# Query norms of a hybrid attention layer: squares of six query tiles of a half folded to 32 channels a head, high and low part summed by one product instead of two

## The chip, the cores and the metric

The kernel runs on one core of a Trainium2 chip. The metric is the device time of one execution in microseconds. TensorE is called PE, VectorE DVE, ScalarE ACT, GpSimd POOL and SyncE SP below; a core has one of each, and each works through its own instructions in order, waiting on semaphores where it needs another.

## The reference, cut to what matters

One layer: 16 meta tokens are put in front of 1024 frames of width 2048, normalised, and multiplied by one input projection of 5376 columns. The queries (16 heads of 64 channels) and keys (2 heads) get an RMSNorm per head, then go into chunked windowed attention; beside it runs a pooling mixer; both are gated and multiplied by an output projection.

```
def _rmsnorm(x, g):
    xf = x.astype(jnp.float32)
    y = xf * lax.rsqrt(jnp.mean(xf * xf, axis=-1, keepdims=True) + EPS)
    return (y * g.astype(jnp.float32)).astype(x.dtype)
...
    q = _rmsnorm(q.reshape(b, l, N_KV_HEADS, GQA_GROUP, HEAD_DIM), q_norm_g)
```

The change touches only the mean over the 64 channels of each query head inside this norm.

## The kernel before, in words

Channels lie on the partitions and frames along the free axis. The frames are worked in two halves of 512 (`h` = 0, 1). In a half, PE computes the projection in tiles of 128 output channels by 512 frames: first keys and values, then the eight query tiles (`PAIRS`, two heads each, called t = 0 to 7 here), then four groups in which attention and the pooling mixer run between further projection tiles. After both halves comes the output projection, which is the second large stage of PE's work.

Every fp32 operand of a product is split into a high part that the fp32r format holds and a low part that is the rest, and a product is the sum of three: high by high, high by low, low by high. The weights arrive in blocks of 128 x 512; a query tile takes four blocks (`TILE_BLKS`), and a block is 12 matmuls (`tile`, lines 1470, 1471, 1477). ACT makes a block's high part (`split_high`, line 630, into `wh`), DVE the low part (`split_low`, line 979, into `wl`), three blocks ahead (`LEAD`), in four buffers, so that the split of block s+3 waits until PE has finished block s-1.

The order of everything in the query stage is written out by hand, on each engine by a loop over s = 0 to 32. Turn s is the turn of block s; the query tile t ends with block 4t+3. What belongs to the norm of tile t hangs on these turns:

- ACT, turn 4t+4: `q_square` reads the finished tile from its PSUM bank twice and writes the squares in fp32 (`q_sq`) and rounded to fp32r (`q_sqh`, in the buffer `d_h`).
- DVE, turn 4t+4, ahead of its `split_low`: `square_low` writes the low part, `q_sq` less `q_sqh`, to `q_sql` (in `d_l`).
- PE, behind block 4t+4: `sum_squares` (lines 1610 and 1611) multiplies both parts by the matrix of ones `ones_r` (it lies in `pw_h`), into the bank `PT` or, for odd t, `PM` (a half of `OP`). A matrix of two 64 x 64 squares of ones gives each channel the sum over its head.
- DVE, turn 4t+5: `q_mean`. ACT, the same turn: `q_sqrt`. DVE, turn 4t+6: `q_norm`, a reciprocal and a product.

PE waits for the low part in front of its sum, and everything behind that wait on PE waits too:

```
                    pe.wait_ge(s_qsl, h * PAIRS + t + 1)
```

Other steps share these turns: on DVE `k_norm` in turn 4 (a reciprocal and one or two products for the keys) and `k_band` in turns 11, 15, 19 and 23 (low parts of the keys); on ACT `k_band` in turns 7 and 14, `v_all_out` in turn 10; on PE the transposes `v_windows` behind block 8, which need `q_norm` of tile 0. Tile 7 is finished in the first turns of the first group.

Of the kernel before, what the change touches and what calls it, by code (L numbers as in the profile page):

```python
# [15 lines left out]
P = 128  # L16
# [15 lines left out]
HD = 64  # L32
PAIRS = 8
# [17 lines left out]
IN_BLKS = KV_BLKS + Q_BLKS + GROUPS * G_BLKS  # L51
ROWT = HALF // P
UNITS = 4

FIRST_SPLITS = ({3: (1, 2), 7: (3, 4), 11: (5, 6), 15: (7,)},
                {3: (3,), 7: (4,), 11: (5, 6), 15: (7,)})
# [27 lines left out]
C_ID, C_BLK, C_MASK = 0, 128, 256  # L84
# [9 lines left out]
def hymba_layer(nc, xcat, norm_g, w_in, w_out, pool_w, vecs, consts, out):  # L94
    f32, f32r, bf16 = mybir.dt.float32, mybir.dt.float32r, mybir.dt.bfloat16
    ACT = mybir.ActivationFunctionType
    ALU = mybir.AluOpType
# [3 lines left out]
    with ctx:  # L101
# [3 lines left out]
        def sem(name):  # L105
            return ctx.enter_context(nc.semaphore(name))
# [8 lines left out]
        cst = sb("cst", [P, C_N])  # L115
# [30 lines left out]
        pw_h = sbi("pw_h", [P, BLK], f32r)  # L146
# [10 lines left out]
        scr = sbi("scr", [P, 7168])  # L157
# [52 lines left out]
        q_sq = [scr[:, 1056:1568], scr[:, 1568:2080]]  # L210
# [3 lines left out]
        q_sqh = [d_h[:, 0, :], d_h[:, 1, :]]  # L214
        q_sql = [d_l[:, 0, :], d_l[:, 1, :]]
        ones_r = pw_h[:, 0:P]
        q_rs = [scr[:, 2080:2592], scr[:, 2592:3104]]

        prob = scr[:, 0:QUAD * KEYS].rearrange("p (c k) -> p c k", c=QUAD)
# [18 lines left out]
        QB = [S[:, 0, :]] + [(R[1][:, :], R[0][:, :], O)[t % 3] for t in range(PAIRS - 1)]  # L238
# [58 lines left out]
        s_pvl = sem("s_pvl")  # L297
        s_qsq = sem("s_qsq")
        s_qsl = sem("s_qsl")
        s_qss = sem("s_qss")  # L300
        s_qsd = sem("s_qsd")
        s_qrs = sem("s_qrs")
# [69 lines left out]
        ME = [ONE + 2 * GROUPS * (h + 1) for h in range(HALVES)]  # L372
        OE = [ONE + GROUPS * UNITS * (h + 1) for h in range(HALVES)]

        OUT_UNITS = HALVES * GROUPS * UNITS

# [29 lines left out]
        def _(sp):  # L406
# [15 lines left out]
            def spill(q):  # L422

                sp.wait_ge(s_me, ONE + 2 * (q + 1))
                sp.wait_ge(s_oe, ONE + UNITS * (q + 1))
                for t in (2 * q, HK + 2 * q):
# [201 lines left out]
        def _(act):  # L628
# [49 lines left out]
            for h in range(HALVES):  # L678
# [104 lines left out]
                def q_square(t):  # L783
                    product_done(act, h, KV_BLKS + t * TILE_BLKS)
                    if t >= 2:
                        act.wait_ge(s_qss, h * PAIRS + t - 1)
                    for dst in (q_sq[t % 2], q_sqh[t % 2]):
                        nc.scalar.activation(dst, QB[t], ACT.Square).then_inc(s_qsq, 1)

                def q_sqrt(t):  # L790
                    if t >= 2:
# [4 lines left out]
                def qdiag(u, g):  # L796

                    act.wait_ge(s_s, ONE + 2 * ((h * GROUPS + g) * UNITS + u))
                    q = mixed[:, bass.ds(PAIRS + g * 2 + u // 2, 1),
# [7 lines left out]
                for s in range(Q_BLKS + 1):  # L807
                    if s and s % 4 == 0:
                        q_square(s // 4 - 1)
                    if s < Q_BLKS:  # L810
                        split_high(h4 + KV_BLKS // RAW, s + LEAD)
                    if s == 0:
                        k_square()
                    if s == 2:
                        r_rows()
                    if s == 3:
                        k_sqrt()
                    if s > 4 and s % 4 == 1:
                        q_sqrt(s // 4 - 1)
                    if s == 10:  # L820
                        v_all_out()
                    if s in (7, 14):
                        k_band((s - 7) // 7)
                    if s == 23:
                        v_operand(0)
                    if s == 30:
                        qdiag(0, 0)
# [139 lines left out]
            for n in range(OUT_BLKS):  # L967
                p, s = divmod(n, PASS)
# [8 lines left out]
        def _(dve):  # L977
# [30 lines left out]
            for h in range(HALVES):  # L1008
# [72 lines left out]
                def k_band(e, i):  # L1081
                    src = slice(e * HD, (e + 1) * HD)

                    high = band_h[src, e, :].rearrange("p (c n) -> p c n", n=BAND)
                    dve.wait_ge(s_kbh, 8 * h + (2, 8)[e])
                    for dst in (slice(i * HD, (i + 1) * HD),):
                        low = band_x[dst, e, :].rearrange("p (c n) -> p c n", n=BAND)
                        sub(low[:, :, 0:CHUNK], kT[src, :].rearrange("p (c n) -> p c n", n=CHUNK),
                            high[:, :, 0:CHUNK])
                        ins = sub(low[:, :, CHUNK:BAND],  # L1090
                                  k_meta[src, :].unsqueeze(1).to_broadcast([HD, NCH + 1, META]),
                                  high[:, :, CHUNK:BAND])
                    if e == 1 and i == 1:
                        ins.then_inc(s_kbl, 1)

                def v_operand(e):
                    dve.wait_ge(s_vh, 3 * (h * KVH + e + 1))
                    sub(v_s[:, :, 1, :], v_all[:, :, e * HD:(e + 1) * HD], v_s[:, :, 0, :])
                    sub(vm[64:64 + META, 0, :], vm_all[:, e * HD:(e + 1) * HD], vm[0:META, 0, :]).then_inc(s_vl, 1)

                def square_low(t):
                    dve.wait_ge(s_qsq, 2 * (h * PAIRS + t + 1))
                    sub(q_sql[t % 2], q_sq[t % 2], q_sqh[t % 2]).then_inc(s_qsl, 1)
# [20 lines left out]
                    sub(qs[HD:P, :, 1, :], q[HD:P], qs[HD:P, :, 1, :]).then_inc(s_qdl, 1)  # L1124

                for s in range(Q_BLKS + 1):
                    if s and s % 4 == 0:
                        square_low(s // 4 - 1)
                    if s < Q_BLKS:
                        split_low(h4 + KV_BLKS // RAW, s + LEAD)  # L1130
                    if s == 1:
                        k_square_low()
                    if s == 3:
                        k_mean()
                        v_out()
                    if s == 4:
                        k_norm()
                    if s > 4 and s % 4 == 1:
                        q_mean(s // 4 - 1)
                    if s > 4 and s % 4 == 2:  # L1140
                        q_norm(s // 4 - 1)
                    if s in (11, 15, 19, 23):
                        k_band((s - 11) // 8, (s - 11) // 4 % 2)
                    if s == 25:
                        v_operand(0)
                    if s == 31:
                        qdiag(0, 0)
# [272 lines left out]
            for i in range(ROWT):  # L1420
                for p in range(PASSES):
                    at = p * PASS + i
# [31 lines left out]
        def _(pe):  # L1454
            mm = nc.tensor.matmul
# [105 lines left out]
            for h in range(HALVES):  # L1561
# [41 lines left out]
                def sum_squares(t):  # L1603
                    pe.wait_ge(s_qsl, h * PAIRS + t + 1)
                    if t == 0:
                        pe.wait_ge(s_ksd, SPANS_BY[h + 1])
                    if t >= 2:
                        pe.wait_ge(s_qsd, h * PAIRS + t - 1)
                    bank = (PT, PM)[t % 2][:, :]
                    mm(bank, ones_r, q_sqh[t % 2], start=True, stop=False)  # L1610
                    mm(bank, ones_r, q_sql[t % 2], start=False, stop=True).then_inc(s_qss, 1)

                def q_events(s):
                    if s == 1:
                        r_transposes()
                    elif s == 2:
                        k_squares()
                    elif s == 8:
                        v_windows()
                    if s and s % 4 == 0:  # L1620
                        sum_squares(s // 4 - 1)

                for t in range(PAIRS):
# [117 lines left out]
            for n in range(OUT_BLKS - LAST):  # L1741
                p, s = divmod(n, PASS)
# [116 lines left out]
```

## Time and profile before

| what | value |
|---|---|
| median of 3 runs | 1175.71 us (1174.88 to 1175.95) |
| the profiled execution's own time | 1175.75 us |
| its span in the trace | 1173.6 us |
| PE busy | 1168.7 us |
| DVE busy | 890.2 us |
| ACT busy | 616.1 us |
| query stage of the first half, by PE's blocks | about 41 to 139 us of the span |

The span is the time from the first to the last instruction in the trace; the execution's own time is 2.1 us more. Busy times are sums over the instructions of an engine. Matmuls overlap: one of 128 x 512 shows 0.39 us, and the next starts about 0.23 us behind it.

### The profile page before, as it was taken

The page shows a single profiled execution, that of the slowest core. Times are in us where ns is not written, and L with a number is a line of the kernel's source. Part 1 is how long each engine was busy: PE and PEld are TensorE (multiplying, and loading weights), DVE is VectorE, ACT ScalarE, POOL GpSimd, SP SyncE. Part 2 cuts the span into 40 slices and gives each one's busy share as a digit, 9 for nine tenths or more (in the row PEclk, how much of TensorE's full clock was granted, in tenths as well). Part 3 has the DMA queues.
Part 4 walks back from the last instruction along what each step waited for, and adds up shares of the span by engine and source line. Part 5 has one row for each costly group of instructions (what it writes and reads, how often), then busy time and mean ns, then how long its engine had stood idle before and what let it go on. Part 6 is the DMA issues. An engine that isn't in the chain of part 4 may idle for free.

```text
span 1173.6 us, 17331 instructions
## 1 busy us (share of the span) xinstructions
PE 1168.7 (100%) x5906; PEld 993.6 (85%) x5906; DVE 890.2 (76%) x1548; ACT 616.1 (53%) x1400; POOL 115.5 (10%) x133
## 2 busy tenths in 40 slices
PE   9999999999999999999999999999999999999999
PEld 8888898898998988888888888888888888888887
DVE  5677878787786885677787787887977977657676
ACT  5654466554665656544564655555654444444442
POOL 0000011030040220000020030220400000200001
PEclk9999999999999999999999999999999999999999
DMA  7255339465385423435268372493246544653443
GB/s 258 82 161 179 90 88 227 121 200 191 120 186 162 126 81 118 156 113 175 88 138 177 90 241 73 102 221 86 85 141 221 167 133 135 187 176 123 142 145 135
DMA packets 85775, 171.41 MB, mean 146 GB/s; under 512 B 8496, under 2 KB 12208, under 8 KB 85552
## 3 DMA queue, kind: packets, MB, share of 16 engines
q1 hardware_dynamic: 72288, 129.21, 35.9%
q0 software_dynamic: 13120, 40.90, 14.2%
q8 instruction: 45, 0.74, 0.3%
q14 instruction: 34, 0.28, 0.1%
q10 hardware_dynamic: 288, 0.28, 0.1%
HBM read 157.77 MB, written 46.14 MB: 174 GB/s over the span
## 4 chain that ended last, share of the span: by engine, by line
PE 99%; DVE 0%; ACT 0%; issue 0%; ACTq 0%; DVEq 0%
PE R L1470 18%; PE R L1471 18%; PE R L1477 18%; PE R L1777 3%; PE R L1778 3%; PE R L1776 3%; PE S L1777 2%; PE S L1778 2%; PE S L1776 2%; PE OP L1777 2%; PE OP L1778 2%; PE OP L1776 2%; PE S L1645 1%; PE OP L1669 1%; PE OP L1477 1%; PE OP L1471 1%
## 5 line engine op out<-in xcount | busy, mean ns | idle before, releaser
L979 DVE TENSOR_TENSOR wl<-raw,wh 128x512 fp32r<-128x512 f32 x384 | 283.4, 739 | 197.8 <-ACT wh L630 196.0
L630 ACT ACTIVATE wh<-raw 128x512 fp32r<-128x512 f32 x384 | 241.0, 629 | 351.5 <-PE R L1477 160.4
L1470 PE MATMUL R<-act_h,wh 128*128 128x512 f32 (+5 forms) x1056 | 380.5, 365 | 0.0
L1471 PE MATMUL R<-act_l,wh 128*128 128x512 f32 (+5 forms) x1056 | 378.5, 364 | 0.0
L1477 PE MATMUL R<-act_h,wl 128*128 128x512 f32 (+5 forms) x1048 | 362.1, 365 | 0.0
L1471 PEld LDWEIGHTS R<-act_l,wh 128*128 128x128 f32 x1056 | 198.5, 188 | 28.6
L1470 PEld LDWEIGHTS R<-act_h,wh 128*128 128x128 f32 x1056 | 198.3, 188 | 28.7
L1477 PEld LDWEIGHTS R<-act_h,wl 128*128 128x128 f32 x1048 | 188.2, 188 | 32.2
L885 ACT ACTIVATE row_buf<-scr 128x512 f32<-128x512 f32 x32 | 20.2, 632 | 79.5 <-DVE scr L1241 79.5
L1183 DVE TENSOR_REDUCE scr<-S 128x288 f32<-128x576 f32 x56 | 42.3, 756 | 25.2 <-PE S L1645 24.3
L1776 PE MATMUL R<-wh,mix_h 128*128 128x512 f32 x152 | 59.1, 389 | 0.0
L1777 PE MATMUL R<-wl,mix_h 128*128 128x512 f32 x152 | 59.1, 389 | 0.0
L1778 PE MATMUL R<-wh,mix_l 128*128 128x512 f32 x152 | 59.1, 389 | 0.0
L1113 DVE RECIPROCAL scr<-scr 128x512 f32<-128x512 f32 x16 | 53.5, 3347 | 0.0
L859 ACT ACTIVATE scr<-scr,nmax 128x144 f32<-128x144 f32 x128 | 51.2, 403 | 3.3 <-DVE nmax L1191 3.3
L600 POOL TENSOR_TENSOR scr<-scr 128x513 f32<-128x513 f32 (+6 forms) x40 | 50.3, 1257 | 3.1
L592 POOL TENSOR_TENSOR scr<-scr,row_buf 128x512 f32<-128x512 f32 (+4 forms) x16 | 20.9, 1304 | 268.3 <-ACT scr L630 258.0
L1776 PE MATMUL S<-wh,mix_h 128*128 128x512 f32 x112 | 43.6, 389 | 0.0
L1777 PE MATMUL S<-wl,mix_h 128*128 128x512 f32 x112 | 43.6, 389 | 0.0
L1778 PE MATMUL S<-wh,mix_l 128*128 128x512 f32 x112 | 43.6, 389 | 0.0
L1776 PE MATMUL OP<-wh,mix_h 128*128 128x512 f32 x104 | 40.5, 389 | 0.0
L1777 PE MATMUL OP<-wl,mix_h 128*128 128x512 f32 x104 | 40.5, 389 | 0.0
(291 smaller groups left out, 1996.2 us busy)
## 6 DMA issues: line engine op xcount, KB each, us to landing
raw<-w_in_blocks SPq DMA_DIRECT2D x271, 256.0 KB, 2.7
wsum<-w_out_in POOLq DMA_DIRECT2D x24, 1024.0 KB, 11.8
raw<-wsum SPq DMA_DIRECT2D x64, 256.0 KB, 2.7
raw<-w_out_in SPq DMA_DIRECT2D x48, 256.0 KB, 3.2
c<-xcat SPq DMA_DIRECT2D x32, 256.0 KB, 3.5
out<-c POOLq DMA_DIRECT2D x28, 256.0 KB, 2.9
mixed<-xcat SPq DMA_DIRECT2D x10, 512.0 KB, 5.5
mx<-mixed SPq DMA_DIRECT2D x8, 512.0 KB, 3.4
```

Of the source, the lines that this page charges most:

```text
L600: ins = pool.tensor_tensor(dst[:, lo:COLS], src[:, lo:COLS], src[:, lo - step:COLS - step], ALU.add)
L630: return nc.scalar.activation(dst, src, ACT.Copy)
L859: nc.scalar.activation(prob[:, c, :], prob[:, c, :], ACT.Exp, bias=nmax[:, c:c + 1], accum_out=den[:, c:c + 1]).then_inc(s_ex, 1)
L979: return nc.vector.tensor_tensor(dst, a, b, ALU.subtract)
L1113: nc.vector.reciprocal(q_rs[t % 2], q_rs[t % 2]).then_inc(s_qrs, 1)
L1183: nc.vector.tensor_reduce(to, both, AX.X, ALU.add).then_inc(s_sm, 1)
L1470: mm(o, wh[:, b, w], xh, start=(k == 0), stop=False)
L1471: mm(o, wh[:, b, w], xl, start=False, stop=False)
L1477: last = mm(o, wl[:, b, w], xh, start=False, stop=(k == KT - 1))
L1776: mm(banks[r], mh, wh[:, slot, :], start=(k == 0), stop=False)
L1777: mm(banks[r], mh, wl[:, slot, :], start=False, stop=False)
L1778: last = mm(banks[r], ml, wh[:, slot, :], start=False, stop=(k == HK - 1))
```

## The change

For the tiles t = 0 to 5 of each half (`FOLDED = 6`) the squares are folded before they are summed. ACT writes the squares of channels 0 to 31 of both heads into a 64-row buffer `q_even`, and those of channels 32 to 63 into another, `q_odd`: four activations of 32 x 512 in place of two of 128 x 512. DVE adds the two (`fold`). ACT copies the 64 x 512 result, rounded to fp32r, into the upper half of `q_sqh` (`fold_high`), and DVE writes the low part into the lower half of the same buffer (`fold_low`). High and low part then lie on the 128 partitions of one operand, and PE takes one product by the matrix `ones_f`, which ACT writes once a half in turn 1 (`ones_folded`). Tiles 6 and 7 stay as they were.

The steps also move: for the folded tiles `fold` and `fold_low` stand in turn 4t+5, PE's sum behind block 4t+5, `q_mean` and `q_sqrt` in turn 4t+6, `q_norm` in turn 4t+7. DVE's `k_band` moves by one turn, to 12, 16, 20 and 24.

```
+FOLDED = 6
...
+        q_even = [q[0:HD] for q in q_sq]
+        q_odd = [scr[0:HD, 5216:5728], scr[0:HD, 5744:6256]]
+        ones_f = pw_h[:, P:2 * P]
...
+                    if t < FOLDED:
+                        for head in range(2):
+                            at = slice(head * 32, (head + 1) * 32)
+                            nc.scalar.activation(q_even[t % 2][at], QB[t][head * HD:head * HD + 32], ACT.Square)
+                            ins = nc.scalar.activation(q_odd[t % 2][at], QB[t][head * HD + 32:(head + 1) * HD], ACT.Square)
+                        ins.then_inc(s_qsq, 2)
+                        return
                     for dst in (q_sq[t % 2], q_sqh[t % 2]):
                         nc.scalar.activation(dst, QB[t], ACT.Square).then_inc(s_qsq, 1)
+
+                def fold_high(t):
+                    act.wait_ge(s_qf, h * FOLDED + t + 1)
+                    copy(q_sqh[t % 2][0:HD], q_even[t % 2]).then_inc(s_qfh, 1)
+
+                def ones_folded():
+                    for to, at in ((0, 0), (32, HD), (HD, 0), (96, HD)):
+                        ins = copy(ones_f[to:to + 32], cst[at:at + 32, C_BLK:C_BLK + P])
+                    ins.then_inc(s_onesf, 1)
...
-                    if s > 4 and s % 4 == 1:
+                    if s == 1:
+                        ones_folded()
+                    if s % 4 == 1 and 0 < s // 4 <= FOLDED:
+                        fold_high(s // 4 - 1)
+                    if s % 4 == 2 and 0 < s // 4 <= FOLDED:
+                        q_sqrt(s // 4 - 1)
+                    elif s % 4 == 1 and s // 4 > FOLDED:
                         q_sqrt(s // 4 - 1)
...
+                def fold(t):
+
+                    dve.wait_ge(s_qsq, 2 * (h * PAIRS + t + 1))
+                    nc.vector.tensor_tensor(q_even[t % 2], q_even[t % 2], q_odd[t % 2], ALU.add).then_inc(s_qf, 1)
+
+                def fold_low(t):
+                    dve.wait_ge(s_qfh, h * FOLDED + t + 1)
+                    sub(q_sqh[t % 2][HD:P], q_even[t % 2], q_sqh[t % 2][0:HD]).then_inc(s_qsl, 1)
...
                 for s in range(Q_BLKS + 1):
-                    if s and s % 4 == 0:
+                    if s % 4 == 0 and s // 4 > FOLDED:
                         square_low(s // 4 - 1)
+                    if s % 4 == 1 and 0 < s // 4 <= FOLDED:
+                        fold(s // 4 - 1)
                     if s < Q_BLKS:
                         split_low(h4 + KV_BLKS // RAW, s + LEAD)
...
-                    if s > 4 and s % 4 == 1:
+                    if s % 4 == 1 and 0 < s // 4 <= FOLDED:
+                        fold_low(s // 4 - 1)
+                    late = s // 4 > FOLDED
+                    if s % 4 == (1 if late else 2) and s > 4:
                         q_mean(s // 4 - 1)
-                    if s > 4 and s % 4 == 2:
+                    if s % 4 == (2 if late else 3) and s > 4:
                         q_norm(s // 4 - 1)
-                    if s in (11, 15, 19, 23):
-                        k_band((s - 11) // 8, (s - 11) // 4 % 2)
+                    if s in (12, 16, 20, 24):
+                        k_band((s - 12) // 8, (s - 12) // 4 % 2)
...
+                    if t < FOLDED:
+                        pe.wait_ge(s_onesf, h + 1)
+                        mm(bank, ones_f, q_sqh[t % 2], start=True, stop=True).then_inc(s_qss, 1)
+                        return
                     mm(bank, ones_r, q_sqh[t % 2], start=True, stop=False)
                     mm(bank, ones_r, q_sql[t % 2], start=False, stop=True).then_inc(s_qss, 1)
...
-                    if s and s % 4 == 0:
+                    if s % 4 == 0 and s // 4 > FOLDED or s % 4 == 1 and 0 < s // 4 <= FOLDED:
                         sum_squares(s // 4 - 1)
```

What this does to the order is best seen in rows. On DVE, in turns 4 and 5 of the first half (tile 0), the kernel before has `square_low` first, then the split of block 7 and the keys' norm (lines 1071 to 1078):

```order
L979 TENSOR_TENSOR d_l<-scr,d_h 128x512 [waits s_qsq]
L979 TENSOR_TENSOR wl<-raw,wh 128x512 [waits s_wh]
L1071 RECIPROCAL scr<-scr 128x528 [waits s_ksd]
L1074 SCALAR_TENSOR_TENSOR k_meta<-scr,vec 128x16 [waits s_krs]
L1078 SCALAR_TENSOR_TENSOR kT<-scr,vec 128x512
L979 TENSOR_TENSOR wl<-raw,wh 128x512 [waits s_wh]
```

The changed kernel has on DVE, in the same two turns, with its own line numbers (1010 is the subtraction, 1135 the fold):

```order
L1010 TENSOR_TENSOR wl<-raw,wh 128x512 [waits s_wh]
L1102 RECIPROCAL scr<-scr 128x528 [waits s_ksd]
L1105 SCALAR_TENSOR_TENSOR k_meta<-scr,vec 128x16 [waits s_krs]
L1109 SCALAR_TENSOR_TENSOR kT<-scr,vec 128x512
L1135 TENSOR_TENSOR scr<-scr 64x512 [waits s_qsq]
L1010 TENSOR_TENSOR wl<-raw,wh 128x512 [waits s_wh]
L1010 TENSOR_TENSOR d_h<-scr,d_h 64x512 [waits s_qfh]
```

What PE's sum waits for stood ahead of the keys' norm and now stands behind it, in two steps with ACT's `fold_high` between them.

On DVE, from turn 11 to 13 of the first half (the norm of tile 1 ends, tile 2's squares begin), the kernel before has:

```order
L979 TENSOR_TENSOR wl<-raw,wh 128x512 [waits s_wh]
L1113 RECIPROCAL scr<-scr 128x512 [waits s_qsd]
L1115 SCALAR_TENSOR_TENSOR mixed<-R,gq,scr 128x512 [waits s_qrs]
L979 TENSOR_TENSOR wl<-raw,wh 128x512 [waits s_wh]
L979 TENSOR_TENSOR band<-kT,band 64x9x64 [waits s_kbh]
L979 TENSOR_TENSOR band<-k_meta,band 64x9x16
L979 TENSOR_TENSOR d_l<-scr,d_h 128x512 [waits s_qsq]
L979 TENSOR_TENSOR wl<-raw,wh 128x512 [waits s_wh] x2
```

The first of these is turn 10's split, and the norm is turn 10's. The changed kernel has on DVE, from turn 11 on:

```order
L1010 TENSOR_TENSOR wl<-raw,wh 128x512 [waits s_wh]
L1153 RECIPROCAL scr<-scr 128x512 [waits s_qsd]
L1155 SCALAR_TENSOR_TENSOR mixed<-R,gq,scr 128x512 [waits s_qrs]
L1010 TENSOR_TENSOR wl<-raw,wh 128x512 [waits s_wh]
L1010 TENSOR_TENSOR band<-kT,band 64x9x64 [waits s_kbh]
L1010 TENSOR_TENSOR band<-k_meta,band 64x9x16
L1135 TENSOR_TENSOR scr<-scr 64x512 [waits s_qsq]
L1010 TENSOR_TENSOR wl<-raw,wh 128x512 [waits s_wh]
L1010 TENSOR_TENSOR d_h<-scr,d_h 64x512 [waits s_qfh]
```

The sequence is the same up to the square's step, but it begins one turn later, with the split of block 14 in place of block 13, and one step of DVE has become two with a wait for ACT between them. Tiles 3, 4 and 5 repeat it.

On ACT, in turns 4 and 5 of the first half (tile 0), the kernel before has:

```order
L788 ACTIVATE scr<-S 128x512 [waits s_blk]
L788 ACTIVATE d_h<-S 128x512
L630 ACTIVATE wh<-raw 128x512 [waits s_blk,s_raw3]
L630 ACTIVATE wh<-raw 128x512 [waits s_blk,s_raw0]
L794 ACTIVATE scr<-scr 128x512 [waits s_qm]
```

The changed kernel has there (799 and 800 are the squares, 639 the copy):

```order
L799 ACTIVATE scr<-S 32x512 [waits s_blk]
L800 ACTIVATE scr<-S 32x512
L799 ACTIVATE scr<-S 32x512
L800 ACTIVATE scr<-S 32x512
L639 ACTIVATE wh<-raw 128x512 [waits s_blk,s_raw3]
L639 ACTIVATE wh<-raw 128x512 [waits s_blk,s_raw0]
L639 ACTIVATE d_h<-scr 64x512 [waits s_qf]
```

Two squares became four, and `fold_high` stands behind both splits, waiting for DVE's fold.

## Rows read from the trace of the kernel before

**Rows 1.** The page: span; busy time, share and count of each engine.

```profile
span 1173.6 us, 17331 instructions
...
PE 1168.7 (100%) x5906; PEld 993.6 (85%) x5906; DVE 890.2 (76%) x1548; ACT 616.1 (53%) x1400; POOL 115.5 (10%) x133
```

**Rows 2.** The waits of PE: line, releaser, us in total, times, longest.

```profile
PE R L1532 <- DVE act_l L991: 0.4, 1, 0.4
```

**Rows 3.** Timeline of PE about block 16 and tile 3's sum: start us, us, instruction.

```profile
86.88 0.39 PE L1470 MATMUL R<-act_h,wh 128*128 128x512 f32 x1
...
89.60 0.39 PE L1610 MATMUL OP<-d_h,pw_h 128*128 128x512 f32 x1
...
90.06 0.39 PE L1470 MATMUL R<-act_h,wh 128*128 128x512 f32 x1
```

**Rows 4.** Timeline of PE behind tile 0, and about `v_windows` behind block 8.

```profile
51.44 0.39 PE L1470 MATMUL R<-act_h,wh 128*128 128x512 f32 x1
...
65.66 0.27 PE L1597 MATMUL R<-cst,v_meta 128*16 128x128 f32 x1
...
66.77 0.50 PE L1610 MATMUL OP<-d_h,pw_h 128*128 128x512 f32 x1
```

**Rows 5.** Timeline of ACT: narrow operations, tile 0's squares, `v_all_out`.

```profile
41.13 0.29 ACT L730 ACTIVATE scr<-xsd 128x128 f32<-128x128 f32 x1
41.33 0.29 ACT L630 ACTIVATE scr<-xrs 16x128 f32<-16x128 f32 x1
...
51.64 0.60 ACT L788 ACTIVATE scr<-S 128x512 f32<-128x512 f32 x1 [0.39 <-PE S L1477]
52.13 0.59 ACT L788 ACTIVATE d_h<-S 128x512 fp32r<-128x512 f32 x1
...
71.04 1.00 ACT L630 ACTIVATE scr<-S 128x1024 f32<-128x1024 f32 x1
```

**Rows 6.** Timeline of DVE in turn 4 of the first half.

```profile
53.36 0.69 DVE L979 TENSOR_TENSOR wl<-raw,wh 128x512 fp32r<-128x512 f32 x1
53.97 3.45 DVE L1071 RECIPROCAL scr<-scr 128x528 f32<-128x528 f32 x1
...
58.26 0.69 DVE L979 TENSOR_TENSOR wl<-raw,wh 128x512 fp32r<-128x512 f32 x1
```

**Rows 7.** Timeline of ACT in turns 14 and 15: splits, and the keys' copies.

```profile
81.70 0.63 ACT L630 ACTIVATE wh<-raw 128x512 fp32r<-128x512 f32 x1 [0.50 <-PE OP L1477]
82.35 0.69 ACT L630 ACTIVATE band<-kT 64x576 fp32r<-64x576 f32 x1
...
84.42 0.63 ACT L630 ACTIVATE wh<-raw 128x512 fp32r<-128x512 f32 x1 [0.25 <-PE OP L1477]
```

**Rows 8.** Timeline of DVE in turns 14 to 16.

```profile
82.97 3.35 DVE L1113 RECIPROCAL scr<-scr 128x512 f32<-128x512 f32 x1
...
87.02 0.68 DVE L979 TENSOR_TENSOR wl<-raw,wh 128x512 fp32r<-128x512 f32 x1
87.73 0.75 DVE L979 TENSOR_TENSOR band<-kT,band 64x576 fp32r<-64x576 f32 x1
...
88.72 0.69 DVE L979 TENSOR_TENSOR d_l<-scr,d_h 128x512 fp32r<-128x512 f32 x1
```

**Rows 9.** The chain between 464 and 467 us: start us, us, what.

```profile
465.39 0.76 DVE act_l L991
```

**Rows 10.** Timeline of PE: its first matmuls, and those behind the wait at 466 us.

```profile
1.47 5.06 PE L1488 MATMUL PT<-pw_l 128*128 128x512 f32 x11 [1.47 <-DVE pw_l L994]
6.33 1.16 PE L1510 MATMUL S<-cst,mixed 128*128 128x128 f32 x8
...
466.19 0.50 PE L1532 MATMUL OP<-act_h,wh 128*128 128x512 f32 x1 [0.17 <-DVE act_l L991]
466.53 0.40 PE L1533 MATMUL OP<-act_l,wh 128*128 128x512 f32 x1
```

**Rows 11.** A stretch: PE, PEld, DVE, ACT, POOL busy; PEclk, DMA share, GB/s.

```profile
0.00:4.00 4.00, 2.53 (x6) 2.05 (x7) 0.48 (x1) 1.51 (x3) 1.50 (x8) 1.00 0.52 148
```

More of the change, by code:

```diff
@@ L299, in hymba_layer @@
         s_qsl = sem("s_qsl")
+        s_qf = sem("s_qf")
+        s_qfh = sem("s_qfh")
+        s_onesf = sem("s_onesf")
         s_qss = sem("s_qss")
```

## The prediction

> **What bounds the kernel now.** The page comes first: PE is busy for 1168.7 of the span's 1173.6 us, DVE for 890.2, ACT for 616.1 [rows 1]. PE's own waits come second: behind its first microseconds the longest is 0.4 us, and the other one there is shorter [rows 2]. So time is won only by taking work from PE, and lost one for one wherever PE must wait, since nothing later on PE has slack that could give a wait back. Third come the timelines of PE, DVE and ACT over the query stage: they show what a product costs, and how late DVE and ACT are when PE asks for the low part of the squares. The profiled execution took 1175.75 us, 0.04 us above the median of the three runs, so the sum below can be set against either.
>
> **What is removed.** Twelve matmuls (tiles 0 to 5 of two halves). The sum of tile 3 begins at 89.60, and the next block at 90.06: two products, 0.23 us each [rows 3]. That it shows 0.39 us is overlap; what counts is from start to start. 12 x 0.227 = 2.7 us, all of it on PE's path. This is the whole possible gain.
>
> **What is added off PE.** For each folded tile ACT has two squares and one 64 x 512 copy more, DVE one subtraction more. None of these lies on PE in itself, but PE's sum waits for the last of them. Their prices: the trace has no 32 x 512 activation. The nearest rows say that time goes by columns and not by partitions: on ACT 16 x 128 and 128 x 128 both take 0.29 us [rows 5], and on DVE 64 x 576 takes 0.75 where 128 x 512 takes 0.69 [rows 6, 8]. So I take full prices: a square 0.49 us from start to start, [rows 5], `fold` and `fold_low` 0.69 us, `fold_high` 0.63 as a 128 x 512 copy (a 64 x 576 one shows 0.69) [rows 7]. The lower bound is that narrow operations cost half: kept for the range. From one engine's end to the next one's start goes 0.03 to 0.04 us: DVE's operation at 465.39 ends at 466.15, and PE starts at 466.19 [rows 9, 10]. Behind such a wait PE's first matmul takes 0.34 us to the next, not 0.23 [rows 10]: 0.11 us more for each wait. The four copies of `ones_folded` (0.2 us each by [rows 5]) fall in front of the split of block 5, three blocks ahead of its use: nothing. The queues of SP and POOL get no new work.
>
> A block is 2.72 us (86.88 to 89.60) [rows 3]. In what follows E is the moment at which PE starts the block behind a tile. PE used to ask for the low part at E + 2.72, and now asks at E + 5.44.
>
> **Tile 0, first half.** E = 51.44 [rows 4], so PE asks at 56.88. ACT starts the squares at 51.64 and has four: 51.64 + 4 x 0.49 = 53.60 [rows 5]. Its split of block 7 ends at 54.23, and DVE's split starts at 54.26. DVE then has the keys' norm, at 54.26 + 0.61 = 54.87; it lasts 4.29 us (53.97 to 58.26) [rows 6], to 59.16. The square's step stood ahead of it; now `fold` stands behind it: 59.16 to 59.85. `fold_high` 59.88 to 60.51, `fold_low` 60.54 to 61.23, PE at 61.27. PE waits 4.39 us. In the second half the keys' norm has no meta columns and is a reciprocal and a product of 512 columns, which elsewhere take 4.05 us (82.97 to 87.02) [rows 8]: 4.15 us.
>
> **Tiles 4 and 5, the plain pattern**, on tile 3's times, E = 86.88, PE asks at 92.32. The norm of the tile before now hangs on turn 4t+3: ACT's split there runs from 84.42 to 85.05 [rows 7], DVE's starts 0.03 later, at 85.08; 0.61 for the split, 4.05 for the norm: 89.74. The split and the keys' band from 87.02 to 88.72 take 1.70 [rows 8]: 91.44. `fold` ends at 92.13, `fold_high` at 92.79, `fold_low` at 93.51, PE at 93.55: a wait of 1.23 us. Before, the norm started one turn earlier, and the low part ran from 88.72 to 89.41 [rows 8], 0.2 us ahead of PE's question at 89.60: the margin was thin already.
>
> **Tiles 2 and 3** add a delay on ACT. A late sum delays `q_mean`, it delays `q_sqrt`, and ACT's turn-10 copies (0.16 + 1.0 us [rows 5]) or turn-14 copies (82.35 to 84.17, 1.8 us [rows 7]) stand behind `q_sqrt` and ahead of the next split, on which DVE's norm hangs. Followed through with the same prices, the split is 0.7 us late for tile 2 and 0.4 us for tile 3: waits of 1.95 and 1.66 us.
>
> **Tile 1** is covered: PE has `v_windows` ahead of its sum, 1.1 us (65.66 to 66.77) [rows 4], and no band work is due; the low part is ready 1.3 us early. But `v_windows` itself needs the norm of tile 0, now in turn 7: PE starts block 7 at 61.27 + 0.34 + 2.72 = 64.33; split on ACT, split on DVE and norm end 5.64 us later at 69.97; PE comes at 69.77 and waits 0.24 us.
>
> **Tile 6** has the old steps, but the norm of tile 5 still ends at E + 2.86 (89.74 less 86.88); `square_low` ends at E + 3.55, PE wanted it at E + 2.72: 0.87 us. Tile 7 is as before.
>
> **The sum.** First half 4.39 + 0.24 + 1.95 + 1.66 + 1.23 + 1.23 + 0.87 = 11.57 us of waiting, and seven restarts at 0.11 = 0.77: 12.3 us. Second half 12.1 us. What the kernel before has of the same kind goes off, about 0.2 us a half (its sum of tile 1 takes 0.33 us to the next matmul). 24.0 - 2.7 = 21.3 us more: 1175.7 + 21.3 = 1197.0 us.
>
> **The clock.** The eleven first matmuls, behind 1.47 us of idleness at the program's start, go from 1.47 to 6.33 us: 0.44 us each, against 0.23 later [rows 3, 10]. These are the durations that the two levels of 1.2 and 2.4 GHz would give, though the granted clock stands at 1.00 there [rows 11]. If PE fell back to that pace behind the two waits of over 4 us, for as many matmuls as at the start, each would cost 11 x (0.44 - 0.23) = 2.4 us. No wait of that length occurs in this trace behind the start, so it can't say. The Trainium skill (TensorE: Matmul & The Clock Gate, "Why this matters for your kernels") tells kernels to leave no long gaps between bursts of matmuls, because the clock then drops to its lower level. By that rule the waits of tile 0, the only long ones, would each be followed by a slow stretch, and the sum would be that of the first rival below; no run here shows it yet.
>
> **The rivals.**
> - *The clock falls too* (0.20). For it speaks the slow start in rows 10; against it that PE is fully busy on both sides of a wait. All of the above plus 2.4 or 4.7 us: 1199.4 to 1201.7.
> - *Narrow operations are cheap* (0.09). If 64 x 512 costs half, `fold`, `fold_high` and `fold_low` save together 1.0 us in each of tiles 0, 2, 3, 4 and 5, in both halves: 10 us less, about 1187. Rows 5 and 8 speak against it.
> - *Not slower* (0.03): PE's wait is not felt, because the low part is there in time after all. That needs `fold` to run ahead of the long DVE operations; then only the removed products count, 1175.7 - 2.7 = 1173.0. It decides where the waits of both halves together stay under 2.7 us, a ninth of what I get; tile 0 alone gives 8.5, and its `fold` stands behind the keys' norm in the program, so I see no way.
> - The forecast itself has 0.68: 1193 to 1199 by itself.
>
> **How the numbers follow.** 1197.0 is the likeliest. A measurement of this kernel tells a change of about 0.2% (2.4 us) from none. Slower by more than that are the forecast, the clock and the cheap case: 0.97. Within: 0.01, faster: 0.02, both out of the third rival. The range, 1191 to 1202, holds the forecast and the clock (0.88) and leaves out the cheap case's centre and the third rival; its lower end allows half of the cheap case's saving (5 us) and a little more for what starts earlier than I followed it.
>
> **What would show it.** PE's waits should have a row for the single product (line 1657) on DVE's `d_h`, ten times or so, over 20 us in all with a longest of 4.2 to 4.4, and one for line 1659 (tile 6) of about 0.9 each half. The product of tile 0 should start at about 61.3 us in place of 54.16, that of tile 3 about 10.7 us later than in the kernel before (2.7 for the block, less 0.7 for three products saved, 8.7 of waits and restarts); stages behind the query stages should keep their lengths. DVE's `fold` of tile 0 should start straight behind the product into `kT`. Blocks behind a wait should still have 0.23 us to a matmul; 0.44 would be the clock. The forecast would be wrong if 64 x 512 operations last near 0.35 us, or if the waits of tiles 2 to 5 fall under 0.5 us.

## The result, and the profile after

The changed kernel takes 1203.16 us (median of six runs, 1202.74 to 1204.6) against 1175.75 us of the kernel before: the ratio is 1.0236, with a 95% interval of 1.0225 to 1.0247. It is 27.4 us slower. The forecast was 1197.0 with a range of 1191 to 1202, so the direction and the waits came as forecast, and the time came out above the range. The profiled execution took 1204.60 us, 28.85 us over that of before.

The page of the changed kernel, span, busy times and granted clock:

```profile
span 1202.5 us, 17365 instructions
...
PE 1173.4 (98%) x5894; PEld 993.7 (83%) x5894; DVE 899.0 (75%) x1560; ACT 640.3 (53%) x1444; POOL 115.5 (10%) x133
...
PEclk9989999999999999899999999999999999999999
```

Beside [rows 1], PE has twelve matmuls fewer (5894 against 5906) and yet is busy 4.7 us longer, with 24 us of new idleness. The clock has a dip in slice 3 and one in slice 17; the two query stages lie there. The waits of PE in the changed kernel (line, releaser, us in total, times, longest), where [rows 2] had nothing over 0.4 us behind the program's start:

```profile
PE PT L1657 <- DVE d_h L1010: 15.3, 6, 4.7
PE OP L1657 <- DVE d_h L1010: 6.3, 4, 1.6
...
PE PT L1659 <- DVE d_l L1010: 1.4, 2, 0.7
PE OP L1718 <- ACT pm L639: 0.8, 1, 0.8
...
PE R L1642 <- DVE mixed L1155: 0.4, 2, 0.2
```

Line 1657 is the single product of a folded tile (even t into `PT`, odd t into `OP`), 1659 the first product of tile 6, 1642 the first value transpose: the places that the forecast named. Ten of the twelve folded tiles make PE wait, tile 1 of each half does not.

Tile 0 of the first half, timeline of DVE:

```profile
54.07 0.69 DVE L1010 TENSOR_TENSOR wl<-raw,wh 128x512 fp32r<-128x512 f32 x1 [3.47 <-ACT wh L639]
...
58.31 0.75 DVE L1109 SCALAR_TENSOR_TENSOR kT<-scr,vec 128x512 f32<-128x512 f32 x1
58.97 0.68 DVE L1135 TENSOR_TENSOR scr<-scr 64x512 f32<-64x512 f32 x1
...
60.34 0.69 DVE L1010 TENSOR_TENSOR d_h<-scr,d_h 64x512 fp32r<-64x512 f32 x1
```

`fold` (line 1135) starts straight behind the product into `kT`, 2.7 us after PE has run out of work. The same place on PE:

```profile
56.00 0.39 PE L1522 MATMUL R<-act_h,wl 128*128 128x512 f32 x1
61.08 0.79 PE L1657 MATMUL PT<-d_h,pw_h 128*128 128x512 f32 x1 [4.70 <-DVE d_h L1010]
61.67 0.63 PE L1515 MATMUL R<-act_h,wh 128*128 128x512 f32 x1
62.10 0.63 PE L1516 MATMUL R<-act_l,wh 128*128 128x512 f32 x1
...
66.37 0.51 PE L1522 MATMUL R<-act_h,wl 128*128 128x512 f32 x1
66.72 0.39 PE L1515 MATMUL R<-act_h,wh 128*128 128x512 f32 x1
```

The next matmul was due at 56.23 and starts at 61.08: 4.85 us lost. (The bracket shows 4.70, because the matmul before it is shown until 56.39; 0.16 us has to be added to every such number.) And then the matmuls stand 0.43 us apart instead of 0.23, for eleven of them. The granted clock in stretches behind it (busy of PE, PEld, DVE, ACT, POOL, then PEclk, DMA share, GB/s):

```profile
51.00:57.00 6.00, 5.39 (x24) 4.13 (x22) 2.93 (x2) 3.50 (x6) 0.00 (x0) 1.00 0.19 61
57.00:61.00 4.00, 0.00 (x0) 0.00 (x0) 3.87 (x6) 1.15 (x2) 0.00 (x0) 0.85 0.00 1
61.00:63.00 2.00, 1.92 (x5) 1.53 (x6) 1.41 (x3) 0.36 (x1) 0.00 (x0) 0.50 0.54 131
...
67.00:70.00 3.00, 3.00 (x15) 2.47 (x14) 2.36 (x2) 2.63 (x6) 0.06 (x1) 1.00 0.17 49
```

1.00 is 2.4 GHz and 0.50 is 1.2 GHz: PE stood still, the clock fell while it did, and came back near 66.4 us. From 61.08 to 66.72 are 5.64 us; at the full clock it would be 0.34 + 12 x 0.227 = 3.06. So 2.6 us are lost to the clock here, and 2.1 us in the same way behind tile 0 of the second half.

Where the 28.85 us lie is seen from equal matmuls. The n-th product of `tile`'s first kind (line 1470 before, 1515 now) is the same work in both kernels; its start in us:

| place | before | changed | later by |
|---|---|---|---|
| start of the first query stage | 38.74 | 38.09 | -0.65 |
| behind it | 141.30 | 155.07 | 13.77 |
| ahead of the second query stage | 481.39 | 495.09 | 13.70 |
| behind it | 586.39 | 614.09 | 27.70 |
| last group, behind the wait on line 1718 | 643.15 | 671.88 | 28.73 |
| near the end of the projections | 853.58 | 882.33 | 28.75 |

The two query stages are 14.42 and 14.00 us longer, and hardly anything (0.07 us) is given back between them.

### The profile page after: what moved, and what is told of

It reads as the page before. It is cut to its first block, busy times and chain, and to the rows that moved or that the text cites. A ratio compares the mean times of both kernels' runs of the same rounds, so it can differ in the third digit from the quotient of the medians.

```text
span 1202.5 us, 17365 instructions
## 1 busy us (share of the span) xinstructions
PE 1173.4 (98%) x5894; PEld 993.7 (83%) x5894; DVE 899.0 (75%) x1560; ACT 640.3 (53%) x1444; POOL 115.5 (10%) x133
## 4 chain that ended last, share of the span: by engine, by line
PE 87%; DVE 8%; ACT 3%; issue 1%; DMA 1%; SPq 0%; ACTq 0%; DVEq 0%
PE R L1515 15%; PE R L1516 15%; PE R L1522 15%; PE R L1826 3%; PE R L1825 3%; PE R L1827 3%; DVE scr L1153 2%; PE S L1826 2%; PE S L1825 2%; PE S L1827 2%; PE OP L1826 2%; PE OP L1825 2%; PE OP L1827 2%; DVE wl L1010 1%; PE S L1694 1%; PE OP L1718 1%
```

## The experiments

Times of the kernel before beside them were 1175.5 to 1175.8 us. All edits are to the changed kernel, but for the last but two, which starts from the kernel before.

**1. The new turns alone.** Nothing is folded; tiles 0 to 5 have the two squares, the low part and the two products of before, in the turns of the changed kernel.

```
 DVE, turn 4t+5:  -fold(t) ... -fold_low(t)   +square_low(t)
 ACT:             -four squares, -fold_high, -ones_folded   +the two squares of before
 PE, behind 4t+5: -one product                +two products
```

> The new turns alone: squares, low part and two products as in the kernel before, but `square_low` in turn 4t+5, the sum behind block 4t+5, the norm in turn 4t+7 and the keys' band one turn later. My theory (the places cost, the fold adds to it): tile 0 still waits, about 2.0 us, because its low part stands behind the keys' norm; tiles 4 and 5 don't wait, since one step instead of three fits in front of PE's question; tiles 2 and 3 wait 0.1 to 0.5, tile 6 about 0.9. Nothing is removed from PE and no wait is long enough to cost clock: 8 to 9 us over the kernel before, 1184.3. If the folding work alone made the loss and the places were harmless: 1175.7.

Measured: 1185.02 us, ratio 1.0078 (1.0061 to 1.0095), 9.2 us more. The waits of its first half, on the timeline of PE:

```profile
58.17 0.50 PE L1642 MATMUL PT<-d_h,pw_h 128*128 128x512 f32 x1 [1.88 <-DVE d_l L999]
68.88 0.27 PE L1629 MATMUL R<-cst,v_meta 128*16 128x128 f32 x1 [0.17 <-DVE mixed L1144]
...
96.54 0.50 PE L1642 MATMUL OP<-d_h,pw_h 128*128 128x512 f32 x1 [0.94 <-DVE d_l L999]
128.94 0.50 PE L1642 MATMUL PT<-d_h,pw_h 128*128 128x512 f32 x1 [0.72 <-DVE d_l L999]
```

Tile 0, tile 3 and tile 6 wait, as expected in place; tile 3 waited longer than expected, tile 2 not at all, and the transposes were not named. One thing the expectation ruled out came: five matmuls behind the wait of tile 0 in the first half the clock fell:

```profile
59.74 0.63 PE L1503 MATMUL R<-act_l,wh 128*128 128x512 f32 x1
60.16 0.63 PE L1509 MATMUL R<-act_h,wl 128*128 128x512 f32 x1
```

That cost 1.6 us in this execution (59.43 to 63.08 us for nine matmuls); two of the four runs list a clock of 1.0, so it does not come every time. A third of the loss comes from the places alone, with no fold in the kernel.

**2. The keys' norm behind the fold of tile 0.**

```
 DVE:  -turn 4: k_norm()
       +turn 5: k_norm(), behind fold_low(0)
```

> The changed kernel with the keys' norm on DVE behind `fold_low` of tile 0 (turn 5) instead of in turn 4. My theory: tile 0's wait of 4.9 us falls to about 0.6 in each half, and with it goes the slow stretch of PE behind it (2.6 and 2.1 us): 13 us less than the changed kernel, 1190. If the wait of tile 0 came from the four squares and the copy on ACT and not from the keys' norm, it would stay above 3 us and the time above 1199.

Measured: 1198.60 us, ratio 1.0198 (1.0181 to 1.0215): 4.6 us less than the changed kernel, not 13. On the timeline of PE:

```profile
56.59 0.50 PE L1657 MATMUL PT<-d_h,pw_h 128*128 128x512 f32 x1 [0.40 <-DVE d_h L1010]
68.27 0.27 PE L1642 MATMUL R<-cst,v_meta 128*16 128x128 f32 x1 [2.99 <-DVE mixed L1155]
```

The wait of tile 0 fell from 4.70 to 0.40 us, as my theory said. But the transposes, which need the norm of tile 0, now wait 2.99 us instead of 0.19 (2.75 in the second half). DVE has the keys' norm and the norm of tile 0, over 8 us, to do between tile 0 and the transposes; the long wait used to give it the time. The theory was right on the cause of the wait and wrong on its worth: most of the wait moved on.

**3. The keys' band behind the fold.**

```
-                    if s in (12, 16, 20, 24):
-                        k_band((s - 12) // 8, (s - 12) // 4 % 2)
+                    if s in (13, 17, 21, 25):
+                        k_band((s - 13) // 8, (s - 13) // 4 % 2)
```

> The changed kernel with DVE's `k_band` one turn later (13, 17, 21, 25), behind `fold_low`. My theory: the fold of tiles 2, 4 and 5 starts 1.1 us earlier and their waits go from 1.7 to 0.6 us; tile 3 gains nothing, since the band work of turn 13 delays `q_mean`, `q_sqrt` and ACT's copies of turn 14 by as much: 6.6 us less than the changed kernel, 1196.6. If DVE were not what is late there (but ACT's copy or the squares), the time would stay at 1203.

Measured: 1197.63 us, ratio 1.0186 (1.0169 to 1.0203), 5.5 us less than the changed kernel. Timeline of PE, tiles 2 to 6 of the first half:

```profile
88.19 0.50 PE L1657 MATMUL PT<-d_h,pw_h 128*128 128x512 f32 x1 [0.68 <-DVE d_h L1010]
...
100.96 0.50 PE L1657 MATMUL OP<-d_h,pw_h 128*128 128x512 f32 x1 [1.37 <-DVE d_h L1010]
...
124.59 0.50 PE L1657 MATMUL OP<-d_h,pw_h 128*128 128x512 f32 x1 [0.41 <-DVE d_h L1010]
134.49 0.50 PE L1659 MATMUL PT<-d_h,pw_h 128*128 128x512 f32 x1 [1.22 <-DVE d_l L1010]
```

Tiles 2, 4 (0.40 us now) and 5 wait 0.9 to 1.1 us less, tile 3 only 0.2 less: that fits the detour through `q_sqrt` and ACT's copies, which was not taken away by itself. Tile 6 got 0.5 us more, which I had not followed.

**4. PE kept busy in the wait of tile 0.**

```
-                    pe.wait_ge(s_qsl, h * PAIRS + t + 1)
                     if t == 0:
                         pe.wait_ge(s_ksd, SPANS_BY[h + 1])
+                        for _ in range(18):
+                            mm(PT[:, :], ones_r, q_sql[0], start=True, stop=True)
+                    pe.wait_ge(s_qsl, h * PAIRS + t + 1)
```

> The changed kernel with 18 matmuls of 128 x 512 more in each half, whose result is thrown away, in front of PE's wait for the low part of tile 0; they take 4.1 of the 4.9 us that PE waits there. Theory of the clock: the matmuls behind the wait take 0.43 us because PE stood still; kept busy, it goes on at 0.23 and the time falls by 2.6 + 2.1 us, to 1198.5, though PE has more work. If the slow stretch had another cause: 1203.

Measured: 1199.30 us, ratio 1.0200 (1.0183 to 1.0217), 3.9 us less than the changed kernel, with 36 matmuls more. Its mean granted clock is 1.0, that of the changed kernel 0.994. Its waits of PE:

```profile
PE PT L1659 <- DVE d_h L1010: 7.2, 6, 1.6
PE OP L1659 <- DVE d_h L1010: 6.3, 4, 1.6
```

What remains of the wait of tile 0 is 0.61 us in the first half and 0.37 in the second, the other waits are as they were, and no slow stretch follows. So the slow matmuls come from PE's standing still.

**5. The fold steps early.** The fold itself is kept.

```
 DVE:  -turn 4t+5: fold(t), split_low, fold_low(t)
       +turn 4t+4: fold(t), fold_low(t), split_low
 ACT:  -turn 4t+5: fold_high(t) behind split_high
       +turn 4t+4: fold_high(t) straight behind the squares
```

> The changed kernel with its own fold, but placed earlier: DVE has `fold` and `fold_low` at the head of turn 4t+4, ahead of the split, the keys' norm and the band, and ACT has `fold_high` straight behind the four squares. PE's sum stays behind block 4t+5, the norm in turn 4t+7. My theory (place, not work): the low part is there 0.5 to 0.8 us before PE asks, in every folded tile; tile 6 still waits 0.9 us and the value transposes 0.35, in both halves. 2.7 us won by the products, 2.5 lost: 1175.3, the same as before. If the chain of three steps itself were too long for the place: waits of 0.5 us and more in tiles 2 to 5, 1181 or more.

Measured: 1197.16 us, ratio 1.0190 (1.0176 to 1.0204). Its waits of PE:

```profile
PE R L1641 <- DVE mixed L1155: 6.9, 2, 3.6
PE PT L1658 <- DVE d_l L1010: 5.1, 2, 2.6
PE OP L1656 <- DVE d_h L1010: 4.4, 4, 2.0
```

The sum of tile 0 no longer waits (the first wait of the stage on PE's timeline is that of the transposes). But the transposes wait 3.6 us, tile 6 2.6 and tile 3 2.0, and the waits of the transposes, in both halves, are followed by matmuls 0.43 us apart (the mean clock is 0.996). My expectation followed each tile from the old lateness of DVE and didn't carry the new one on: DVE stands idle while ACT makes the high part, and both engines start their next steps later by that. The time went to the waits of things behind the sum.

**6. The fold steps and the norm early.** As 5, and:

```
-                    if s % 4 == (2 if late else 3) and s > 4:
+                    if s % 4 == 2 and s > 4:
                         q_norm(s // 4 - 1)
```

> As the kernel with the early fold, and DVE's `q_norm` of the folded tiles one turn earlier (4t+6, behind `q_mean`). My theory: that also takes away the waits of tile 6 and of the value transposes, so that the removed products remain: 1173.0, 2.7 us under the kernel before. If DVE's idle wait for ACT's square root inside turn 4t+6 makes something else late: 1175 or more.

Measured: 1186.26 us, ratio 1.0097 (1.0083 to 1.0110): 10.9 us under 5, far from 1173.0. Its waits of PE:

```profile
PE R L1641 <- DVE mixed L1155: 4.7, 2, 2.5
PE PT L1658 <- DVE d_l L1010: 4.0, 2, 2.0
```

Tiles 0 to 4 are free of waits. What is left sits mainly at both ends of the folded run; beside it tile 5 of the first half waits 1.0 us, behind a weight block for which ACT had waited 2.6 us (at 110.80), and tile 5 of the second half, where the same block comes 1.1 us sooner (at 546.22, 5.06 us behind tile 4's sum instead of 6.19), does not wait. At its start the keys' norm ends at 60.5 us and that of tile 0 at 67.1, with PE at the transposes at 64.8. At its end tile 6 asks one block earlier than a folded tile does, while the mean of tile 5 still stands a turn later than in the kernel before, with its norm behind it.

**7. Narrow squares that change no partitions.** Half of the channels are left out of the squares; the times of the steps are what it is for.

```
-   activation(q_even[t % 2][at], QB[t][head * HD:head * HD + 32], ACT.Square)
-   activation(q_odd[t % 2][at], QB[t][head * HD + 32:(head + 1) * HD], ACT.Square)
+   activation(q_even[t % 2][at], QB[t][at], ACT.Square)
+   activation(q_odd[t % 2][at], QB[t][at], ACT.Square)
```

> The changed kernel, but the four narrow squares read the same 32 partitions that they write (channels 0 to 31 into both buffers for head 0, 32 to 63 for head 1), so half the channels are left out of the squares and none is moved between partitions. In the changed kernel a square follows the other at 0.60 us and not at 0.49. Theory A: the move to other partitions costs it; then 0.49 here and about 3 us less than the changed kernel, 1200. Theory B: the change of start partition from one operation to the next, or their narrowness, costs it: 1203, with at most one of the gaps shorter.

Measured: 1202.96 us, ratio 1.0231 (1.0217 to 1.0245), the same as the changed kernel within the interval. Tile 4's squares, timeline of ACT, first in the changed kernel:

```profile
108.15 0.59 ACT L799 ACTIVATE scr<-R 32x512 f32<-32x512 f32 x1 [2.03 <-PE R L1522]
108.74 0.59 ACT L800 ACTIVATE scr<-R 32x512 f32<-32x512 f32 x1
109.34 0.59 ACT L799 ACTIVATE scr<-R 32x512 f32<-32x512 f32 x1
109.95 0.59 ACT L800 ACTIVATE scr<-R 32x512 f32<-32x512 f32 x1
```

and in this one:

```profile
108.08 0.59 ACT L799 ACTIVATE scr<-R 32x512 f32<-32x512 f32 x1 [2.03 <-PE R L1522]
108.58 0.57 ACT L800 ACTIVATE scr<-R 32x512 f32<-32x512 f32 x1
109.16 0.59 ACT L799 ACTIVATE scr<-R 32x512 f32<-32x512 f32 x1
109.66 0.57 ACT L800 ACTIVATE scr<-R 32x512 f32<-32x512 f32 x1
```

Where the next square starts at the same partitions it follows at 0.50 us, where it starts at others at 0.58 to 0.60. So theory B holds: the change of start partition costs 0.1 us, not the narrowness and not the move. (In the changed kernel the first two squares of a head write to the same partitions and differ only in where they read, so a change of the input's start is enough.) Two gaps of three became shorter, where the expectation had one. The times can't tell the kernels apart, but the traces can: the waits of tiles 0, 4 and 5 fell by 0.24 to 0.25 us in both halves (tile 4 from 1.51 to 1.27), those of tiles 2 and 3 did not.

**8. The gain by itself**, from the kernel before. The low part of tiles 0 to 5 is left out of the sum.

```
+                    if t < 6:
+                        mm(bank, ones_r, q_sqh[t % 2], start=True, stop=True).then_inc(s_qss, 1)
+                        return
                     mm(bank, ones_r, q_sqh[t % 2], start=True, stop=False)
```

> The kernel before with one of the two products left out in tiles 0 to 5 of each half (the low part is not summed there), and nothing else changed. It prices the gain: twelve matmuls of 0.227 us, 2.7 us less, 1173.0. If the product lay in PE's idle time anyway: 1175.7.

Measured: 1173.60 us (eleven runs), ratio 0.9985 (0.9976 to 0.9994): 0.7 to 2.8 us less. The forecast 2.7 lies in it, and there is no more to win than that. By equal matmuls in the profiled executions the two query stages are 1.19 and 1.17 us shorter, 2.4 us in all.

**9. Tile 0 put back alone.** Tiles 1 to 5 stay folded, in the new turns.

```
 fold, fold_high, fold_low, one product, late mean and norm:
-                    0 < s // 4 <= FOLDED
+                    1 < s // 4 <= FOLDED
```

> The changed kernel with tile 0 alone put back: its squares, low part, two products, mean and norm are done as in the kernel before and in their old turns; tiles 1 to 5 stay folded, in the new turns. My theory: the wait of 4.9 us, the slow matmuls behind it and the wait of the value transposes go, the waits of tiles 2 to 6 stay at 1.7, 1.75, 1.7, 1.7 and 0.9: about 6.9 us a half over the kernel before, 1189.5. Unlike the kernel that only moved the keys' norm behind the fold, this one has less DVE work ahead of the norm of tile 0. If the wait is bound to move on again (to the transposes), as it did there: 1195 or more.

Measured: 1192.12 us, ratio 1.0139 (1.0124 to 1.0155), 11.0 us less than the changed kernel. The transposes don't wait at all. The 2.6 us over my number sit in tile 2 of the first half, on the timeline of PE:

```profile
83.10 0.50 PE L1657 MATMUL PT<-d_h,pw_h 128*128 128x512 f32 x1 [2.99 <-DVE d_h L1010]
83.44 0.39 PE L1515 MATMUL OP<-act_h,wh 128*128 128x512 f32 x1
83.66 0.57 PE L1516 MATMUL OP<-act_l,wh 128*128 128x512 f32 x1
84.03 0.63 PE L1522 MATMUL OP<-act_h,wl 128*128 128x512 f32 x1
```

and, for its cause, ACT's split of block 14 there:

```profile
74.17 0.63 ACT L639 ACTIVATE wh<-raw 128x512 fp32r<-128x512 f32 x1 [1.31 <-DMA raw<-w_in_blocks]
```

A weight block landed 1.3 us late, the wait of tile 2 is 1.4 us longer than in the changed kernel, and the clock fell behind it. In the second half of the same execution no block is late there, and tile 2 waits 1.57 us, as in the changed kernel. The kernel before had late blocks too, and they cost it nothing.

**10. Five folded tiles, with free places.** Tile 0 as in 9, both fold steps as in 5, the norm as in 6, and:

```
-                    if s in (12, 16, 20, 24):
+                    if s in (11, 15, 19, 23):
...
-                    if s == 25:
+                    if s == 28:
                         v_operand(0)
```

> The version that the runs so far point to: tiles 1 to 5 folded (tile 0 as in the kernel before), both fold steps in turn 4t+4 ahead of the split, ACT's copy straight behind the squares, the norm of a folded tile in turn 4t+6, the keys' band back in turns 11, 15, 19 and 23, DVE's `v_operand` in turn 28 instead of 25. Followed through with the durations measured so far, no low part is late and no wait is left that the kernel before doesn't have. Ten products fewer: 2.3 us less than the kernel before, 1173.3. If a wait is left somewhere that I don't see: each costs its length, and 1176 or more would mean that folding has no free place in this stage.

Measured: 1174.14 us (eleven runs, 1173.16 to 1174.75), ratio 0.9988 (0.9979 to 0.9997): 1.45 us under the kernel before, and 29 us under the changed one. Its waits of PE for a low part:

```profile
PE OP L1656 <- DVE d_h L1010: 1.0, 1, 1.0
...
PE PT L1658 <- DVE d_l L1010: 0.2, 1, 0.2
```

The 1.0 us is tile 5 of the first half. ACT waited 3.2 us for a weight block just before it, at 108.38 us. In the second half the same block comes 2.4 us sooner (at 536.91, 3.77 us behind tile 4's sum instead of 6.16), and tile 5 does not wait. That fits the difference to the 2.3 us that were hoped for; that the late block is the cause was not tried by itself.

How much of the 1.45 us the folding gives, the times alone don't show. By equal matmuls in the profiled executions the first query stage is 0.51 us longer than in the kernel before, with tile 5's wait in it, and the second 1.11 us shorter, which is the whole price of five products (5 x 0.227 = 1.14). Another 0.70 us lie ahead of the first query stage, and there the executions differ by up to 0.9 us among themselves; experiment 8, whose program is the same there, begins that stage 0.56 us earlier than the kernel before.

## Why the prediction was right and wrong

- **What bounds, and the sign.** Right. PE is the bound, no wait on it was given back later (13.77 us behind the first query stage, 13.70 ahead of the second), and the waits came where they were placed: tile 0, the transposes, tiles 2 to 6, and not tile 1. Experiments 2, 3 and 9 take away a single cause each, and the wait named for it shrinks.
- **The gain.** Right: twelve products, 2.7 us; experiment 8 measured 1.9 (0.7 to 2.8), and 2.4 by its trace.
- **Tile 0.** Named right, 4.39 forecast and 4.85 measured (second half 4.15 and 4.61). The term that was mis-sized is "a square 0.49 us from start to start": it was read from squares that all start at partition 0. Four squares take 2.41 us, not 1.96 (experiment 7). In the sum of both halves this term is 0.9 us here and 1.8 in tiles 4 and 5.
- **Tiles 4 and 5.** 1.23 forecast, 1.67 measured (1.51 shown), by the same term. With squares of 0.49 us ACT's split would have been ready when DVE came; with 0.60 DVE's split waits for ACT's. This is a step that the forecast passed over, since it took DVE alone as late there. Experiment 7 bears it out: squares 0.23 us shorter in all, waits of tiles 4 and 5 0.24 and 0.25 shorter.
- **Tiles 2, 3 and 6, the transposes.** Forecast 1.95, 1.66, 0.87 and 0.24; measured 1.73, 1.75, 0.88 and 0.35. Close, though the way through `q_sqrt` and ACT's copies was only partly tested (experiment 3).
- **Narrow operations cheap.** Ruled out: `fold` and `fold_low` show 0.68 to 0.69 us, `fold_high` 0.63, the prices that were taken.
- **The clock.** This is the step that failed. It stood as a rival with a chance of 0.20, priced at 2.4 us for each half, and stood at nothing in the sum. It came, at 2.6 and 2.1 us. What the prediction set against it, that PE is fully busy on both sides of a wait, did not keep it away: PE is fully busy on both sides of tile 0's wait, and the clock fell. Experiment 4 shows the cause: the same wait filled with matmuls keeps the clock at 1.0, and the time falls by 3.9 us. The Trainium skill (TensorE: Matmul & The Clock Gate, "Why this matters for your kernels") tells kernels to leave no long idle gaps between bursts of matmuls. That rule spoke for the rival, and the waits of 4.85 and 4.61 us bear it out. That the kernel before has no long wait to show it was no evidence against it.
- **The range.** The clock alone would have stayed in it (1201.7 against an upper end of 1202). It was left because the mis-sized squares came on top, 2.7 us, for which the upper end had nothing over. With the clock's loss taken away, experiment 4 measured 1199.3, against 1197.0 + 2.7 = 1199.7.

**The balance of the profiled execution.** Forecast 21.3 us more. Waits of both halves 25.6 instead of 22.9: +2.7. The clock: 2.6 + 2.1 = +4.7. Together 28.7 for the two query stages, which measure 14.42 + 14.00 = 28.4. (A measured wait is the number in brackets and 0.16 us; tiles 0 and 2 to 6 and the transposes of a half give 12.9 and 12.7 us.) The rest of the 28.85 us was in no forecast, and nearly cancels: the start of the program took 0.65 us less (PE's first eleven matmuls give way to the next at 5.81 us instead of 6.33, as among the other runs, where it is 5.55 to 6.33), and a wait in a group of the second half, line 1718 for ACT, cost 1.03. Just ahead of that wait ACT waited for a late weight block:

```profile
657.65 0.63 ACT L639 ACTIVATE wh<-raw 128x512 fp32r<-128x512 f32 x1 [0.95 <-DMA raw<-w_in_blocks]
```

The profiles of experiments 6 and 7 have both the late block there (1.00 and 0.84 us) and the wait; the other eight, and that of before, have neither. So that wait goes with a late block and not with the fold; why the block is late in some executions stays open. The median of the six runs is 1.4 us below the profiled one; the runs list granted clocks of 0.994 to 0.997, so the clock's loss varies from run to run.

## What to carry to other kernels

Where one engine is busy all the time, price a change by the question "at what moment does it ask, and at what moment is the answer there", tile by tile. Twelve matmuls saved were worth 2.7 us, and three dependent steps across two engines, queued behind a long reciprocal, cost ten times that. When such a wait is taken away, follow the engine behind it on to the next consumer: experiments 2 and 5 removed the wait that they were made for and found much of it again at the transposes or at the first tile of the old kind; experiment 6 only shortened those two. And a wait of some microseconds on TensorE should be booked with the slow matmuls behind it, not without: in these traces every wait of 3.0 us or more behind the program's start had them.

## What the hardware showed that I had not expected

- The clock fell not only behind waits of 4.5 us and more. In experiment 1 it fell behind one of 1.9 us (and held over the 1.6 us of the second half), in experiment 6 behind one of 2.0 us (tile 6, first half), in the first half of experiment 2 behind one of 3.0 us, and in 9 behind one of 3.0 us, there only after the first two matmuls had gone at full speed. It held 1.00 over the 2.0 us of tile 6 in the second half of experiment 6, over the 2.5 and 2.2 us of its transposes, and over 2.75 us in the second half of experiment 2. The timeline of PE in experiment 6, behind tile 6's wait in the first half:

```profile
127.66 0.53 PE L1658 MATMUL PT<-d_h,pw_h 128*128 128x512 f32 x1 [2.01 <-DVE d_l L1010]
128.00 0.62 PE L1659 MATMUL PT<-d_l,pw_h 128*128 128x512 f32 x1
128.41 0.63 PE L1514 MATMUL R<-act_h,wh 128*128 128x512 f32 x1
```

  So whether a wait of 1.9 to 2.75 us costs clock can't be told from its length in these runs. What else decides it stays open.
- On ScalarE, an operation whose start partition differs from that of the one before it follows at 0.58 to 0.61 us instead of 0.50 (32 x 512, experiment 7 and the changed kernel).
- The same kind of late weight block cost nothing in one order of steps and a wait of PE in another. ACT waits 2.67, 1.62 and 2.37 us for blocks in the query stages of the kernel before, and PE has no wait behind them; in experiments 6, 9 and 10 one tile each waits behind such a block, and the same tile of the other half, where that block comes sooner, waits less or not at all.
